# Start offsets inside the SBUF tensors that TensorE reads: weight parts, down activations and attention outputs of a two-layer decoder trunk

## The reference

```
for l in range(DEPTH):
    x = x + 0.5 * swiglu(rms_norm(x, ffn1_norm[l]), ffn1_w_gate[l], ffn1_w_up[l], ffn1_w_down[l])
    h = rms_norm(x, mix_norm[l])
    proj = h @ w_in[l]
    ...                      # sliding-window attention o_a, latent attention o_b
    merged = sigmoid(g_a) * (o_a @ w_branch_a[l]) + sigmoid(g_b) * (o_b @ w_branch_b[l])
    x = x + merged @ w_out[l]
    x = x + 0.5 * swiglu(rms_norm(x, ffn2_norm[l]), ffn2_w_gate[l], ffn2_w_up[l], ffn2_w_down[l])
swiglu(x, g, u, d) = (silu(x @ g) * (x @ u)) @ d      # hidden width 2816 = 22 blocks of 128
```

## Time and profile before

| | |
|---|---|
| median of 3 runs | 1042.05 us (1040.8 to 1042.1) |
| the profiled execution, its own time | 1040.86 us |
| its span, first to last instruction | 1039.1 us |
| PE busy | 1034.3 us, 5648 matmuls |
| DVE busy, ACT busy | 718.2 us, 586.2 us |
| mean bandwidth of the transfers | 180 GB/s |

### The profile page before, as it was taken

One profiled execution on the slowest core, in us unless ns is written; L12 is line 12 of the kernel. 1 busy time (PEld: TensorE's weight loads), 2 busy tenths in 40 slices (PEclk: granted clock), 3 DMA queues, 4 the chain that ended last, 5 costly groups with the idle time before them and its releaser, 6 DMA issues.

```text
span 1039.1 us, 15559 instructions
## 1 busy us (share of the span) xinstructions
PE 1034.3 (100%) x5648; PEld 892.9 (86%) x5648; DVE 718.2 (69%) x1132; ACT 586.2 (56%) x935; POOL 61.7 (6%) x71
## 2 busy tenths in 40 slices
PE   9999999999999999999999999999999999999998
PEld 8888888998888888888888888889988888888887
DVE  7766676668786866666687666666688868676665
ACT  7545454557964655454565455454678646454552
POOL 0052000121100000000000000001211000000000
PEclk9999999999999999999999999999999999999999
DMA  7765554455335555655545555634454346545551
GB/s 268 255 230 178 202 167 161 146 187 197 132 123 203 183 191 181 213 182 203 183 152 197 197 201 180 211 133 151 151 204 162 122 162 223 202 164 200 191 172 61
DMA packets 35269, 187.53 MB, mean 180 GB/s; under 512 B 4368, under 2 KB 4384, under 8 KB 20128
## 3 DMA queue, kind: packets, MB, share of 16 engines
q1 hardware_dynamic: 34992, 186.51, 51.6%
q0 software_dynamic: 240, 0.53, 0.2%
HBM read 185.98 MB, written 1.05 MB: 180 GB/s over the span
## 4 chain that ended last, share of the span: by engine, by line
PE 99%; DMA 0%; ACT 0%; DVE 0%; issue 0%; ACTq 0%
PE ps L1369 96%; PE ps L1803 1%; PE ps L1393 1%; PE ps L1832 1%; DMA x_cols<-in_x_first 0%; PE ps L1868 0%; PE ps L1712 0%; ACT hT L610 0%; PE ps L1704 0%; PE ps L1414 0%; DVE x_cols L999 0%; ACT w_hi L554 0%; PE ps L1402 0%; ACTq L609 0%
## 5 line engine op out<-in xcount | busy, mean ns | idle before, releaser
L1369 PE MATMUL ps<-hT,w_hi 128*128 128x512 f32 x1408 | 341.6, 391 | 0.1
L1369 PEld LDWEIGHTS ps<-hT,w_hi 128*128 128x128 f32 x1408 | 258.9, 188 | 51.7 <-ACT w_hi L554 0.4
L884 DVE TENSOR_TENSOR w_lo<-w_raw,w_hi 128x2048 fp32r<-128x2048 f32 x82 | 188.0, 2293 | 87.3 <-ACT w_hi L549 87.3
L1369 PEld LDWEIGHTS ps<-hT,w_lo 128*128 128x128 f32 x1408 | 177.9, 188 | 6.9
L1369 PE MATMUL ps<-hT,w_lo 128*128 128x256 f32 x1408 | 179.7, 279 | 0.0
L1369 PE MATMUL ps<-w_hi,hT 128*128 128x512 f32 (+2 forms) x576 | 174.3, 377 | 0.0
L549 ACT ACTIVATE w_hi<-w_raw 128x2048 fp32r<-128x2048 f32 x85 | 161.9, 1905 | 13.5 <-PE ps L1369 13.2
L1369 PE MATMUL ps<-w_hi,aTl 128*128 128x512 f32 x352 | 137.1, 389 | 0.0
L1369 PE MATMUL ps<-w_lo,aTh 128*128 128x512 f32 x352 | 137.1, 389 | 0.0
L1369 PE MATMUL ps<-w_hi,aTh 128*128 128x512 f32 x352 | 136.8, 391 | 0.0
L578 ACT ACTIVATE S<-ps 128x256 f32<-128x256 f32 x88 | 33.8, 384 | 157.3 <-PE ps L1369 157.3
(11 more groups left out here) (168 smaller groups left out, 953.1 us busy)
## 6 DMA issues: line engine op xcount, KB each, us to landing
w_raw<-in_w_ffn SPq DMA_DIRECT2D x85, 1024.0 KB, 5.0
w_raw<-in_w_ffn SPq DMA_DIRECT2D x90, 512.0 KB, 5.7
w_raw<-in_w_gate SPq DMA_DIRECT2D x16, 1024.0 KB, 5.2
w_raw<-in_w_proj SPq DMA_DIRECT2D x16, 592.0 KB, 4.6
w_raw<-in_w_branch SPq DMA_DIRECT2D x8, 1024.0 KB, 4.8
w_raw<-in_w_out SPq DMA_DIRECT2D x8, 1024.0 KB, 4.9
w_raw<-in_w_uq SPq DMA_DIRECT2D x4, 384.0 KB, 3.0
w_raw<-in_w_ffn SPq DMA_DIRECT2D x4, 256.0 KB, 5.2
```

Of the source, the lines that this page charges most:

```text
L884: dve.tensor_tensor(wl_gu[b], raw_gu[b], wh_gu[b].bitcast(F32), ALU.subtract).then_inc(lo_gu.sem, 1)
L1369: return pe.matmul(dst, w, m, start=start, stop=stop, skip_group_check=True)
```

## The change

The tensors get room in front, and the slices that TensorE reads begin at other bytes of them:

- `w_hi` is as wide as `w_lo` (slots 2176 columns apart instead of 2048). The high parts of gate and up begin 60 columns (240 bytes) into slot 0 and 62 columns (248 bytes) into slot 1, instead of 0.
- The low parts of gate and up begin 60 columns (240 bytes) into slot 0 and 52 columns (208 bytes) into slot 1, instead of 112 (448 bytes) in both.
- `aTh` and `aTl` become two parts of one tensor `aT`, from column 127 (508 bytes) of it on; `oTh` and `oTl` two parts of `oT`, from column 126 (504 bytes) on.

The down weights, all slots of the mixing stage, `hT`, and the order and number of instructions are as before. What is added to the tensors is a multiple of 512 bytes each time (1536, 512 and 512), so every tensor keeps its remainder by 512.

```diff
-LO_SHIFT = 112
-LO_SLOT = GU_COLS + 128
+HI_SHIFT, LO_SHIFT = (60, 62), (60, 52)
+PART_SLOT = GU_COLS + 128
...
+AT_SHIFT, OT_SHIFT = 127, 126
...
-        w_hi = sb("w_hi", [P, MIX_SLOTS * GU_COLS], F32R)
-        w_lo = sb("w_lo", [P, MIX_SLOTS * LO_SLOT], F32R)
-        raw_gu, wh_gu = ([w[:, i * GU_COLS:(i + 1) * GU_COLS] for i in range(2)] for w in (w_raw, w_hi))
-        wl_gu = [w_lo[:, i * LO_SLOT + LO_SHIFT:i * LO_SLOT + LO_SHIFT + GU_COLS] for i in range(2)]
...
+        w_hi = sb("w_hi", [P, MIX_SLOTS * PART_SLOT], F32R)
+        w_lo = sb("w_lo", [P, MIX_SLOTS * PART_SLOT], F32R)
+        raw_gu = [w_raw[:, i * GU_COLS:(i + 1) * GU_COLS] for i in range(2)]
+        wh_gu, wl_gu = ([w[:, i * PART_SLOT + at:i * PART_SLOT + at + GU_COLS] for i, at in enumerate(shifts)]
+                        for w, shifts in ((w_hi, HI_SHIFT), (w_lo, LO_SHIFT)))
...
-        aTh = sb("aTh", [P, 2, SEQ], F32R)
-        aTl = sb("aTl", [P, 2, SEQ], F32R)
+        aT = sb("aT", [P, 128 + 4 * SEQ], F32R)
+        aTh, aTl = (aT[:, AT_SHIFT + i * 2 * SEQ:AT_SHIFT + (i + 1) * 2 * SEQ].rearrange("p (b n) -> p b n", b=2) for i in range(2))
...
-        oTh = sb("oTh", [P, 8, SEQ], F32R)
-        oTl = sb("oTl", [P, 8, SEQ], F32R)
+        oT = sb("oT", [P, 128 + 16 * SEQ], F32R)
+        oTh, oTl = (oT[:, OT_SHIFT + i * 8 * SEQ:OT_SHIFT + (i + 1) * 8 * SEQ].rearrange("p (b n) -> p b n", b=8) for i in range(2))
```

More of the change, by code:

```diff
@@ L110, in build @@
         w_raw = sb("w_raw", [P, MIX_SLOTS * GU_COLS])
-        w_hi = sb("w_hi", [P, MIX_SLOTS * GU_COLS], F32R)
-        w_lo = sb("w_lo", [P, MIX_SLOTS * LO_SLOT], F32R)
-        raw_gu, wh_gu = ([w[:, i * GU_COLS:(i + 1) * GU_COLS] for i in range(2)] for w in (w_raw, w_hi))
-        wl_gu = [w_lo[:, i * LO_SLOT + LO_SHIFT:i * LO_SLOT + LO_SHIFT + GU_COLS] for i in range(2)]
[L115 to L119, removed]
+        w_hi = sb("w_hi", [P, MIX_SLOTS * PART_SLOT], F32R)
[3 more added lines that the diff above has]
+                        for w, shifts in ((w_hi, HI_SHIFT), (w_lo, LO_SHIFT)))
+        raw_d = [w_raw[:, 2 * GU_COLS + i * DN_COLS:2 * GU_COLS + (i + 1) * DN_COLS] for i in range(2)]
+        wh_d, wl_d = ([w[:, 2 * PART_SLOT + i * DN_COLS:2 * PART_SLOT + (i + 1) * DN_COLS] for i in range(2)]
+                      for w in (w_hi, w_lo))
+        mix_raw = [w_raw[:, i * GU_COLS:(i + 1) * GU_COLS] for i in range(MIX_SLOTS)]
+        mix_hi, mix_lo = ([w[:, i * PART_SLOT:i * PART_SLOT + GU_COLS] for i in range(MIX_SLOTS)] for w in (w_hi, w_lo))
         hT = sb("hT", [P, KC, 2, SEQ], F32R)
         hTh, hTl = hT[:, :, 0, :], hT[:, :, 1, :]
-        aTh = sb("aTh", [P, 2, SEQ], F32R)
-        aTl = sb("aTl", [P, 2, SEQ], F32R)
+        aT = sb("aT", [P, 128 + 4 * SEQ], F32R)
+        aTh, aTl = (aT[:, AT_SHIFT + i * 2 * SEQ:AT_SHIFT + (i + 1) * 2 * SEQ].rearrange("p (b n) -> p b n", b=2) for i in range(2))
         work = sb("work", [P, 4 * SEQ])
```

## The result

The changed kernel takes 1046.1 us (median of 3 runs, 1045.74 to 1046.62) against 1042.05 us before: 4.05 us slower, a ratio of 1.0045 with a 95% interval of 1.0031 to 1.0058. The forecast was 1036.0.

The account below looks back on a forecast made before the run. PE was taken as the bound, through the distance of matmul starts. 2.2 ns on each of 2728 matmuls gave 6.0 us, low parts and writes 0: 1042.05 - 6.0 = 1036.0 us; range 1032 to 1040, 8 in 10 1012 to 1048.

Parts of the forecast that it names:

- What bounds the kernel: Whole span: PE busy 1034.3 of 1039.1 us, 99% of the chain, so only the distance between matmul starts can move time.
- The excess belongs to the change of the stationary tile: All matmuls: time beside one column per cycle, 13.3 ns wide and 11.1 in low parts, is paid for changing tile, not streaming.
- a thin basis: High parts, down, attention outputs: shifted starts take the low parts' 11.1 ns instead of 13.3, 2.2 x 2728 = 6.0 us gained.
- Low parts at 0: Low parts of gate and up, 1408 matmuls: already off and staying off, so 0 us change; bounds 3.9 gained, 3.1 lost.
- 256 bytes change nothing: Branch products, tiles 256 bytes apart, take 226.7 ns like aligned ones, so new offsets count as 4 to 48 bytes short.
- Writes at new bytes cost nothing: ACT and DVE writes: a shifted write costs 5 ns, counted as nothing against 5.8 us of DVE idle time per turn.
- No change: Rival, all matmuls: the excess is a fixed price of changing the stationary tile wherever it lies; 1042 us, chance 0.22.
- the transposes: Transposes of `x` (64 bytes off against `ident`) and `S` (not off) both last 272 ns, cited for the no-change rival.
- a read port of its own for the weight load: Skill rule: loading the next tile takes nothing from the running matmul, so start addresses can't matter; 1042 us.
- The rule of lines of 16 bytes: Tiles 4 or 8 bytes off touch 33 lines instead of 32: 0.4 ns on 2024 matmuls, 0.8 us lost.
- Much faster: Rival, shifted matmuls: reads of next stationary and moving tiles clash, offset parts them; 26 us gained, 1016 us, chance 0.20.
- Slower: Rival, shifted families: they stay at 232.2 ns instead of settling at 226.7; 15 us lost, 1057 us, chance 0.20.

Follow-up runs that it names:

- the map: Decoder left out: 48 matmuls at each of 64 stationary starts, 0 to 252 bytes short; 226.9 ns at 0 wide, 120.0 at 0 narrow.
- six forerunners: Decoder left out: 48 wide matmuls at seven stationary starts, each after six kinds of preceding matmuls; 508 takes 226.7 ns after aligned wide, 233.5 after narrow at 448.
- the second map: Decoder left out, stationary tile fixed, moving tile 0 to 252 bytes short; wide 236.6 ns at 8 short, 230.0 at 4 short.

## Why the prediction was wrong

*What bounds the kernel* was right: PE alone, and only the distance of starts could move.

*The excess belongs to the change of the stationary tile, and an offset can lower it*: half right. That it belongs to the change of tile is not shown: no run keeps one tile for several matmuls. For narrow matmuls the map shows 120.0 ns at 0 and 117.8 at 64 short, an excess of 13.3 and 11.1, just the two numbers of the argument.

*The step that failed* is the one called a thin basis: carrying the 2.2 ns of the narrow low parts over to the 2728 wide matmuls. A narrow matmul has starts that are better than the aligned one; a wide one has none among 64, and at 8 bytes short it rests at 233.3 instead of 226.7. What the prediction took as 6.0 us gained was a loss in the high parts and attention outputs, and nothing in down.

*Low parts at 0*: right as a sum (117.8 before and after), but by luck, since one slot went to 118.8 and the other to 116.9, and for the wrong reason. They were expected to stay because being off was what counted; in fact their place decides between 113.3 and 120 ns, and so does what ran before them.

*256 bytes change nothing*: right where it was tried; the pairs 508 and 252, 504 and 248, 496 and 240 have the same values.

*Writes at new bytes cost nothing*: right, DVE and ACT did not move.

*The rivals.* "No change" fell: the transposes, read as a sign that 64 bytes do nothing, said nothing of these matmuls. Its rule from the Trainium skill, page "TensorE: Matmul & The Clock Gate" (Part 2, first step), a read port of its own for the weight load, doesn't make starts harmless: with the other engines still, the stationary start alone takes the distance from 226.9 to 242.8 ns. The rule of lines of 16 bytes in the Trainium skill, page "SBUF — State Buffer" (Door 1), doesn't sort them either: 4 bytes short, across a line, can cost nothing, and 16 short, on a line, costs 1.6 ns after narrow matmuls at 448. "Much faster" fell: no shifted wide family went under the 226.7 ns of the aligned ones. "Slower" had the right sign and the right word, rest points: it said that a run of equals rests at 226.7 only for starts that agree. It was wrong in two things. The shifted families do settle, only higher, at 233.3; and that holds for some starts, not for all that disagree, so that 4 us came of its 15.

What remains open is why a start has the rest points that it has. Shifting either tile changes the distance, and so does what ran before; no other engine is needed. That the reads of the two tiles clash in SBUF would fit, but no run here shows it.

## What to carry to other kernels

Where PE is never idle, read the distance of matmul starts, not their lengths, and compare it with columns over clock: what is left beside is worth a map of its own, one short kernel with all starts in one run. Measure a start in the place where it will stand, with what runs before it; alone it may rest elsewhere. An offset that helps one width need not help another, and for wide matmuls the aligned start was the safe one here, of the seven places tried with six forerunners the only one that always came to 226.7 ns.

## What the runs showed that I had not expected

A run of equal matmuls can rest at several distances. Where a run settles at one value, that value is nearly always one of a few: 226.7, 230.0, 233.3 and 240.0 ns for 512 columns (240.0 with the moving tile 28 bytes short, (108.67 - 100.99) / 32; 230.0 with the stationary one 156 short, (464.98 - 457.62) / 32), and 113.3, 116.7 and 120.0 for 256. The steps are multiples of 3.3 ns, which is 8 columns at 2.4 GHz. Three narrow starts of the second map, at 115.6, fit no such step, and many other starts do not settle at one value but repeat a pattern of several.

And one start moved from 0 to 4 bytes short, that of the down activations, made the low parts of gate and up 4 ns faster, at a start that nobody had touched, for as long as the loop ran.
